# Storing a block's output from the residual's buffer, and transposing the next block's first chunk one half tile sooner

## The chip, the cores and the metric

The kernel runs on one core of a Trainium2 chip. Its time is device time in microseconds. The kernel before takes 1905.79 us, the median of three runs (1905.21 to 1907.05). A TensorE matmul of the granted full clock (2.4 GHz) is the unit in which most of the time goes.

## The reference

One layer of a hybrid decoder block over 4096 positions with 1024 channels, float32, batch 1:

```
h    = rms_norm(x, norm_g) * (1 + scale(c)) + shift(c)      # adaLN
proj = h @ w_in                                             # u, z_pool, q, k, v, o, z, gates
pool = (trailing means over 2/4/8/16 of u, minus u) @ w_pool * ls * silu(z_pool)
q, k = silu(causal conv of width 4)
hm   = mLSTM(q, k, v, gates), 4 heads of 128, chunks of 128 positions, in sequence
mix  = concat(pool, rms_norm(hm) * mh_norm_g * sigmoid(o) * silu(z))
out  = rms_norm(x + gate(c) * (mix @ w_out), final_g)
```

## The kernel before

The sequence is cut into 8 blocks of 512 positions, and a block into 4 chunks of 128. Block 0 is written out by itself (it also splits the weights), blocks 1 to 6 are a loop, and block 7 is written out again, without preparing a next one. Every large product is made in three matmuls from operands split into a high and a low part (`split3`, L465 to L469). Each engine has its own instruction list, in the order in which the code is written; semaphores order the engines among each other. All DMAs are issued by SP, one after another, so a DMA that waits keeps back those written behind it.

A block goes like this. TensorE computes v and the gates from eight units of weights (`v_part`), first four units for the first two chunks, then the rest; the second part waits until the last low part of the block's input is there (`h_lo`). Then come 16 tiles (q, k, z, o), of 24 matmuls each, in the accumulators acc0 and acc1 by turns, and then, per chunk, the pool tiles u and zp between the mLSTM's small products. VectorE's part of a chunk is `heads(j)` (it divides numerator by denominator and signals `h_ready`), `update_c(j)`, `head_var`, `head_norm`, and for the pool branch `y_low` (signals `y_lo`).

The output stage of a block has eight half tiles (chunk j, 512 of the 1024 columns each). `out_m(i)` adds the 12 matmuls of the mLSTM half, `out_p(i)` the 12 of the pool half, into the accumulator i % 2. `out_m(i)` waits until VectorE has emptied it (`acc_free`). Between them `prep_next(p)` transposes half a chunk of the next block's input (4 transposes) from `x_in` into num0 or num1; its first call waits for `h_ready` of chunk 3, because `heads(3)` reads these banks. VectorE then runs `add_residual(i)` (accumulator plus the loaded input row, into `x_res`), `prep_full` (scale and shift of the transposed chunk), `prep_var` and `prep_scale` for the next input chunk, `out_var(j)` and `out_norm(j)`. ScalarE squares, GpSimd takes the root. ScalarE (L748) and GpSimd (L966) split the prepared chunk into high and low.

`x_in` and `x_res` hold two chunks each. `load_x(b+1, c)` fills `x_in` when the transposes of chunk c-2 are done (`x_T`). `load_res(b, j)` fills `x_res[j % 2]` with the input rows of chunk j, and `store(b, j)` writes the normed chunk out. At the end of a block SP has, in this order: weights for the next block, `load_x(2)`, `store(0)`, one unit of weights, `load_x(3)`, `load_res(2)`, `store(1)`, `load_res(3)`, `store(2)`, `store(3)`. The normed chunk lies in `normed`, which is the memory of qT: q is no longer needed then, and the next block's first q tile waits until the stores are through.

Of the kernel before, what the change touches and what calls it, by code (L numbers as in the profile page):

```python
# [34 lines left out]
P = 128  # L35
# [3 lines left out]
BLK = 512  # L39
NB = SEQ // BLK  # L40
NC = BLK // P
# [59 lines left out]
def build(nc, x, c, norm_g, w_ada, b_ada, w_in, b_gates, conv_w, conv_b, w_pool, ls_pool, mh_norm_g,  # L101
# [3 lines left out]
    with ExitStack() as ctx:  # L105
        def sb(name, shape, dt=F32):
            return ctx.enter_context(nc.sbuf_tensor("sb_" + name, shape, dt))
# [4 lines left out]
        def sem(name):  # L112
            return ctx.enter_context(nc.semaphore(name))
# [13 lines left out]
        qT, kT, oz = sb("qT", [P, NH, BLK]), sb("kT", [P, NH, BLK]), sb("oz", [P, NH, BLK])  # L127
# [11 lines left out]
        x_in = sb("x_in", [P, 2, D])  # L139
        x_res = sb("x_res", [P, 2, D])  # L140
        full = [dmat, k_w]
        normed = qT[:, :, :].rearrange("p (a h) n -> p a (h n)", a=2)
        junk = tanh[:, :].bitcast(BF16)
        fg = sb("fg", [P, D])
        wpool = q_in
# [28 lines left out]
        o_sq, o_var, o_rs = sb("o_sq", [P, 2]), sb("o_var", [P, 2]), sb("o_rs", [P, 2])  # L174
# [56 lines left out]
        stored = [sem("stored0"), sem("stored1")]  # L231
        o_sq_done, o_var_done, o_rs_done, o_ready = (
            sem("o_sq_done"), sem("o_var_done"), sem("o_rs_done"), sem("o_ready"))
# [10 lines left out]
        def reach(eng, sem, value):  # L244

            if not (isinstance(value, int) and value <= 0):
                eng.wait_ge(sem, value)
# [34 lines left out]
        def _(sp):  # L282
# [65 lines left out]

            def load_res(b, j):

                reach(sp, o_ready, b * NC + (j - 1))
                sp.dma_start(x_res[:, j % 2, :], x[0, bass.ds(b * BLK + j * P, P), :]).then_inc(res_loaded[j % 2], 16)

            def store(b, j):
                sp.wait_ge(o_ready, b * NC + (j + 1))
                sp.dma_start(out[0, bass.ds(b * BLK + j * P, P), :], normed[:, j % 2, :]).then_inc(stored[j % 2], 16)

            sp.dma_start(cst[:, :], consts[:, 0:K_END]).then_inc(cst_loaded, 16)
            sp.dma_start(warm[:, :, :].rearrange("p g n -> p (g n)"), consts[:, K_END:K_END + K_COR]).then_inc(misc_loaded, 16)
# [104 lines left out]
        def _(pe):  # L464
# [52 lines left out]
            def one_block(b, last_block, first=False):  # L517
                def acc_wait(name, i):
                    t = TASK[name, i]
                    reach(pe, acc_free[t % 2], b * (TASKS // 2) + t // 2)  # L520
                    return acc[t % 2]
# [158 lines left out]
                def out_m(i):  # L680

                    j, cols = i // 2, slice(512 * (i % 2), 512 * (i % 2) + 512)
                    dst = acc_wait("out", i)
                    if first and i == 0:
                        pe.wait_ge(wout_lo_done, KT)
                    if i % 2 == 0:
                        pe.wait_ge(m_lo, b * NC + (j + 1))
                    for h in range(NH):
                        split3(dst[:, :], mixm_hi[:, j % 2, h, :], mixm_lo[:, j % 2, h, :],
                               wo_hi[:, NH + h, cols], wo_lo[:, NH + h, cols], h == 0, False)  # L690
# [12 lines left out]
                def prep_next(p):  # L703
                    if not last_block:
                        if p == 0:
                            pe.wait_ge(h_ready, b * NC + NC)
                        prep(b + 1, p)

                out_m(0)
                out_m(1)  # L710
                prep_next(0)
                prep_next(1)
                for i in range(8):
                    if i > 1:
                        out_m(i)
                    out_p(i)
                    if i == 1:
                        hm_transposed(3)
                    if i in (2, 4, 6):
                        prep_next(i)  # L720
                        prep_next(i + 1)
# [298 lines left out]
        def _(dve):  # L1020
            V = nc.vector
# [4 lines left out]
            def step(ins):  # L1026

                ins.then_inc(dve_step, 1)
                count[0] += 1
                did(dve_step, base[0] + count[0])  # L1030
# [5 lines left out]
            def in_turn():  # L1036

                reach(dve, *latest[0])
# [128 lines left out]
            def one_block(b, last_block, first=False):  # L1167
# [112 lines left out]
                for t, (name, i) in enumerate(TILES[:16]):  # L1280
                    in_turn()
                    if name in "qk":

                        sh = shifted[:, t % 2, :]
                        tap = [par[:, C_CW + 8 * n + t:C_CW + 8 * n + t + 1] for n in range(CW)]
                        step(V.tensor_copy(sh[:, HALO - 3:HALO], halo_qk[:, t, :]))
                        dve.wait_ge(acc_free[t % 2], b * (TASKS // 2) + (t // 2 + 1))
                        step(V.tensor_scalar(acc_cv[:, HALO:], sh[:, HALO:], tap[3], par[:, C_CB + t:C_CB + t + 1],
                                             ALU.mult, ALU.add))
                        for n in (2, 1, 0):  # L1290
                            in_turn()
                            ins = V.scalar_tensor_tensor(acc_cv[:, HALO:], sh[:, HALO - 3 + n:HALO - 3 + n + BLK], tap[n],  # L1292
                                                         acc_cv[:, HALO:], ALU.mult, ALU.add)
                            if n:
                                step(ins)
                            else:
                                ins.then_inc(conv_done, 1)
                                did(conv_done, b * 8 + (t + 1))
                        V.tensor_copy(halo_qk[:, t, :], sh[:, HALO + BLK - 3:HALO + BLK]).then_inc(shifted_free, 1)
                        dve.wait_ge(tanh_ready, b * TANHS + (t + 1))  # L1300
                        dve.wait_ge(conv_done, b * 8 + (t + 1))
                        if t == 0:
                            for i2 in range(2):
                                reach(dve, stored[i2], 16 * 2 * b)
                        V.scalar_tensor_tensor((qT if name == "q" else kT)[:, i, :], tanh[:, :], 1.0, acc_cv[:, HALO:],
                                               ALU.add, ALU.mult).then_inc(qk_ready, 1)
                        did(qk_ready, b * 8 + (t + 1))
                    elif name == "z":

                        src, free = acc_wait(name, i)  # L1310
                        dve.wait_ge(tanh_ready, b * TANHS + (t + 1))
                        V.scalar_tensor_tensor(oz[:, i, :], tanh[:, :], 1.0, src[:, :], ALU.add, ALU.mult).then_inc(free, 1)  # L1312
                        did(free, b * (TASKS // 2) + (TASK[name, i] // 2 + 1))
                    else:

                        src, free = acc_wait(name, i)
                        dve.wait_ge(tanh_ready, b * TANHS + (t + 1))
                        V.tensor_tensor(oz[:, i, :], tanh[:, :], oz[:, i, :], ALU.mult).then_inc(free, 1)  # L1318
                        did(free, b * (TASKS // 2) + (TASK[name, i] // 2 + 1))
                    if t == 0:  # L1320
                        log_gates()
                    if t == 2:
                        running_max()
                    if t == 4:
                        maxima()
                    if t == 6:
                        exponents()
                    if t == 8:
                        wide_rows()
                    if first and t > WOUT_TILE and t - WOUT_TILE <= KT:  # L1330
                        wout_low(t - WOUT_TILE - 1)
                    if first and 0 <= t - WOUT_TILE < KT:
                        wout_scale(t - WOUT_TILE)
                    if first and 0 <= t - FOLD_TILE - 1 < 2 * NH:
                        f = t - FOLD_TILE - 1
                        in_turn()
                        dve.wait_ge(fold_hi, f + 1)
                        V.tensor_tensor(mixm_lo[:, f % 2, :, :], num[1][:, :].rearrange("p (k n) -> p k n", n=P),
                                        mixm_hi[:, f % 2, :, :].bitcast(F32), ALU.subtract).then_inc(fold_lo, 1)
                        did(fold_lo, f + 1)  # L1340
# [174 lines left out]
                def out_norm(j):  # L1515
                    in_turn()
                    dve.wait_ge(o_rs_done, b * NC + (j + 1))
                    reach(dve, stored[j % 2], 16 * (b * 2 + j // 2))
                    V.scalar_tensor_tensor(normed[:, j % 2, :], x_res[:, j % 2, :], o_rs[:, j % 2:j % 2 + 1], fg[:, :],  # L1519
                                           ALU.mult, ALU.mult).then_inc(o_ready, 1)  # L1520
                    did(o_ready, b * NC + (j + 1))

# [58 lines left out]
```

## Time and profile before

| | |
|---|---|
| median of three runs | 1905.79 us |
| the profiled execution | 1905.21 us, its span 1903.4 us |
| TensorE matmul busy | 1819.3 us, 96% |
| TensorE weight load busy | 1552.0 us, 82% |
| VectorE busy | 1077.3 us, 57% |
| ScalarE busy | 470.2 us, 25% |
| GpSimd busy | 236.4 us, 12% |
| DMA, moved over the span | 324.32 MB, 170 GB/s |

Busy time is the union of an engine's instructions; matmuls overlap, so 96% says that there is nearly always one under way. The setup takes the first slices of the span; from then on one block follows another every 224 us, and the blocks 1 to 6 look alike. Output stages end near 331, 555, 780, 1004, 1229, 1453, 1677 and 1900 us. Times of rows are microseconds from the start of the span.

### The profile page before, as it was taken

Reading aid. Unit: us, or ns where it says so; the run is one execution under the profiler, and the core shown is the slowest. Engines: PE = TensorE matmul, PEld = TensorE weight load, DVE = VectorE, ACT = ScalarE, POOL = GpSimd, SP = SyncE. Lnnn points to the kernel's source line nnn. Section 1 sums busy time; section 2 is a strip of 40 time slices with the busy share of each in tenths; the row PEclk is TensorE's granted clock in tenths of the full one; section 3 lists DMA queues with packets and bytes.
Section 4 is the critical chain, followed back from the end, with each engine's and each line's share of the span. In section 5 each row is a group of like instructions: output and inputs, shape, how many; then the busy total and the mean of one; then the engine's idle time right before and its main releaser. Section 6 shows DMA issues by size and latency. Waiting matters only on the chain.

```text
span 1903.4 us, 27224 instructions
## 1 busy us (share of the span) xinstructions
PE 1819.3 (96%) x9505; PEld 1552.0 (82%) x9505; DVE 1077.3 (57%) x2453; ACT 470.2 (25%) x970; POOL 236.4 (12%) x213
## 2 busy tenths in 40 slices
PE   2797999999999999999999999999999999999998
PEld 1676888988888888888889888888888888898886
DVE  7677586454745366372764637544573627646373
ACT  1134432212312122221222122221221212222221
POOL 0443213000120002100020000300012000210000
PEclk9999999999999999999999999999999999999999
DMA  9598952665235652456425563266524564256521
GB/s 298 172 302 266 308 182 78 203 195 201 90 134 190 203 183 80 156 188 210 152 72 188 189 201 121 89 209 191 194 74 163 189 212 150 87 170 193 169 100 67
DMA packets 131499, 324.32 MB, mean 170 GB/s; under 512 B 11724, under 2 KB 49316, under 8 KB 131364
## 3 DMA queue, kind: packets, MB, share of 16 engines
q1 hardware_dynamic: 131364, 322.53, 51.3%
q8 instruction: 84, 1.38, 0.3%
q14 instruction: 51, 0.42, 0.1%
HBM read 276.28 MB, written 46.20 MB: 169 GB/s over the span
## 4 chain that ended last, share of the span: by engine, by line
issue 53%; PE 17%; DVE 14%; DMA 7%; POOL 2%; ACT 2%; SPq 1%; DVEq 0%; POOLq 0%; ACTq 0%
PE ps_acc L467 5%; PE ps_acc L469 4%; PE ps_acc L468 4%; DMA w_kept<-sb_w_split 2%; DMA sb_x_in<-x 2%; DVE sb_dmat L1063 2%; DVE sb_k_w L1063 2%; DVE sb_x_res L1505 1%; DMA sb_x_res<-x 1%; DVE sb_qT L1519 1%; POOL sb_h_rs L972 1%; DVE sb_mixm_lo L1418 1%; DVE sb_x_in L1045 1%; DMA sb_w_raw<-w_in 1%; POOL sb_hT_lo L966 1%
## 5 line engine op out<-in xcount | busy, mean ns | idle before, releaser
L467 PE MATMUL ps_acc<-sb_hT_hi,sb_w_split 128*128 128x512 f32 x1536 | 603.7, 393 | 0.0
L468 PE MATMUL ps_acc<-sb_hT_lo,sb_w_split 128*128 128x512 f32 x1536 | 599.5, 390 | 0.0
L469 PE MATMUL ps_acc<-sb_hT_hi,sb_w_split 128*128 128x512 f32 x1536 | 599.5, 390 | 0.0
L469 PEld LDWEIGHTS ps_acc<-sb_hT_hi,sb_w_split 128*128 128x128 f32 x1536 | 289.0, 188 | 61.6
L468 PEld LDWEIGHTS ps_acc<-sb_hT_lo,sb_w_split 128*128 128x128 f32 x1536 | 289.2, 188 | 59.2
L467 PEld LDWEIGHTS ps_acc<-sb_hT_hi,sb_w_split 128*128 128x128 f32 x1536 | 289.5, 188 | 58.5 <-POOL sb_w_split L960 0.3
L972 POOL TENSOR_TENSOR sb_h_rs<-sb_h_var,sb_mhalf 128x4 f32<-128x4 f32 x32 | 32.4, 1013 | 1122.5 <-DVE sb_h_var L1384 1122.5
L1292 DVE SCALAR_TENSOR_TENSOR sb_acc_cv<-sb_shifted,sb_par,sb_acc_cv 128x512 f32<-128x512 f32 x192 | 146.2, 762 | 6.8
L467 PE MATMUL ps_acc<-sb_wo_hi,sb_mixm_hi 128*128 128x512 f32 x256 | 103.8, 406 | 3.7 <-DVE sb_x_res L1505 3.7
L1318 DVE TENSOR_TENSOR sb_oz<-sb_tanh,sb_oz 128x512 f32<-128x512 f32 x32 | 22.2, 693 | 147.1 <-ACT sb_tanh L856 147.1
L467 PE MATMUL ps_acc<-sb_wo_hi,sb_mixp_hi 128*128 128x512 f32 x256 | 100.4, 392 | 3.3 <-DVE sb_mixp_lo L1403 3.3
L469 PE MATMUL ps_acc<-sb_wo_hi,sb_mixm_lo 128*128 128x512 f32 x256 | 100.1, 391 | 0.0
L468 PE MATMUL ps_acc<-sb_wo_lo,sb_mixm_hi 128*128 128x512 f32 x256 | 99.8, 390 | 0.0
L469 PE MATMUL ps_acc<-sb_wo_hi,sb_mixp_lo 128*128 128x512 f32 x256 | 99.8, 390 | 0.0
L468 PE MATMUL ps_acc<-sb_wo_lo,sb_mixp_hi 128*128 128x512 f32 x256 | 99.6, 389 | 0.0
L846 ACT ACTIVATE sb_tanh<-sb_acc_cv 128x512 f32<-128x512 f32 x64 | 40.6, 634 | 171.5 <-DVE sb_acc_cv L1292 171.4
L960 POOL TENSOR_TENSOR sb_w_split<-sb_w_raw,sb_w_split 128x512 fp32r<-128x512 f32 (+1 forms) x48 | 66.1, 1380 | 128.7 <-ACT sb_w_split L739 128.7
L467 PE MATMUL ps_kv<-sb_w_split,sb_hT_hi 128*128 128x256 f32 x256 | 73.0, 285 | 6.8 <-POOL sb_w_split L960 3.9
L1505 DVE TENSOR_TENSOR sb_x_res<-ps_acc,sb_x_res 128x512 f32<-128x512 f32 x64 | 44.3, 692 | 62.2 <-PE ps_acc L469 40.0
L1192 DVE TENSOR_TENSOR sb_g_pre<-ps_sco,sb_bg 128x8 f32<-128x8 f32 x8 | 1.3, 167 | 128.0 <-PE ps_num L469 128.0
L1312 DVE SCALAR_TENSOR_TENSOR sb_oz<-sb_tanh,ps_acc 128x512 f32<-128x512 f32 x32 | 22.0, 689 | 90.4 <-ACT sb_tanh L852 90.3
L875 ACT ACTIVATE sb_tanh<-sb_hm 128x128 bf16<-128x128 f32 x128 | 38.2, 300 | 139.9 <-DVE sb_hm L1366 139.9
(220 smaller groups left out, 2950.1 us busy)
## 6 DMA issues: line engine op xcount, KB each, us to landing
sb_w_split<-w_kept SPq DMA_DIRECT2D x344, 512.0 KB, 3.6
sb_w_split<-w_kept SPq DMA_DIRECT2D x56, 520.0 KB, 4.1
w_kept<-sb_w_split SPq DMA_DIRECT2D x40, 512.0 KB, 5.9
sb_x_res<-x SPq DMA_DIRECT2D x34, 512.0 KB, 5.6
out<-sb_qT SPq DMA_DIRECT2D x32, 512.0 KB, 2.9
sb_x_in<-x SPq DMA_DIRECT2D x30, 512.0 KB, 5.8
sb_w_raw<-w_in SPq DMA_DIRECT2D x48, 256.0 KB, 4.5
w_kept<-sb_w_split SPq DMA_DIRECT2D x8, 520.0 KB, 4.8
```

The lines of the kernel that those rows point to most:

```text
L467: pe.matmul(dst, st_hi, mv_hi, start=start, stop=False)
L468: pe.matmul(dst, st_hi, mv_lo, start=False, stop=False)
L469: return pe.matmul(dst, st_lo, mv_hi, start=False, stop=stop)
L846: act.activation(tanh[:, :], acc_cv[:, HALO:], ACT.Tanh, scale=0.5).then_inc(tanh_ready, 1)
L875: last = act.activation(junk[:, chunk(h)], hm[:, h, :], ACT.Square, accum_out=h_sq[:, h:h + 1])
L960: nc.gpsimd.tensor_tensor(w_split[:, m % RING, lo], w_raw[:, m % RING, lo], w_split[:, m % RING, hi].bitcast(F32), ALU.subtract).then_inc( ...
L972: nc.gpsimd.tensor_tensor(dst, src, mhalf[:, 0:n], ALU.pow).then_inc(done, 1)
L1063: last = V.tensor_scalar(full[p % 2][:, i, :], num[p % 2][:, chunk(i)], gain[:, k:k + 1], shift[:, k:k + 1], ALU.mult, ALU.add)
L1292: ins = V.scalar_tensor_tensor(acc_cv[:, HALO:], sh[:, HALO - 3 + n:HALO - 3 + n + BLK], tap[n], acc_cv[:, HALO:], ALU.mult, ALU.add)
L1312: V.scalar_tensor_tensor(oz[:, i, :], tanh[:, :], 1.0, src[:, :], ALU.add, ALU.mult).then_inc(free, 1)
L1318: V.tensor_tensor(oz[:, i, :], tanh[:, :], oz[:, i, :], ALU.mult).then_inc(free, 1)
L1505: V.tensor_tensor(x_res[:, j % 2, s], src[:, :], x_res[:, j % 2, s], ALU.add).then_inc(free, 1)
```

## The change

The normed chunk is written back into `x_res`, and the stores read it there. `load_res(b, j)` now waits until the store of the chunk two before it has landed (`stored`), where it waited for that chunk's norm (`o_ready`). VectorE's waits for `stored` are gone, in `out_norm` and at the first q tile. On TensorE `prep_next(0)` and `prep_next(1)` stand ahead of `out_m(1)`.

```
-        normed = qT[:, :, :].rearrange("p (a h) n -> p a (h n)", a=2)
...
             def load_res(b, j):
-                reach(sp, o_ready, b * NC + (j - 1))
+                reach(sp, stored[j % 2], 16 * (b * 2 + j // 2))
                 sp.dma_start(x_res[:, j % 2, :], x[0, bass.ds(b * BLK + j * P, P), :]).then_inc(res_loaded[j % 2], 16)

             def store(b, j):
                 sp.wait_ge(o_ready, b * NC + (j + 1))
-                sp.dma_start(out[0, bass.ds(b * BLK + j * P, P), :], normed[:, j % 2, :]).then_inc(stored[j % 2], 16)
+                sp.dma_start(out[0, bass.ds(b * BLK + j * P, P), :], x_res[:, j % 2, :]).then_inc(stored[j % 2], 16)
...
                 out_m(0)
-                out_m(1)
                 prep_next(0)
                 prep_next(1)
+                out_m(1)
                 for i in range(8):
                     if i > 1:
                         out_m(i)
                     out_p(i)
...
                         dve.wait_ge(tanh_ready, b * TANHS + (t + 1))
                         dve.wait_ge(conv_done, b * 8 + (t + 1))
-                        if t == 0:
-                            for i2 in range(2):
-                                reach(dve, stored[i2], 16 * 2 * b)
...
                 def out_norm(j):
                     in_turn()
                     dve.wait_ge(o_rs_done, b * NC + (j + 1))
-                    reach(dve, stored[j % 2], 16 * (b * 2 + j // 2))
-                    V.scalar_tensor_tensor(normed[:, j % 2, :], x_res[:, j % 2, :], o_rs[:, j % 2:j % 2 + 1], fg[:, :],
+                    V.scalar_tensor_tensor(x_res[:, j % 2, :], x_res[:, j % 2, :], o_rs[:, j % 2:j % 2 + 1], fg[:, :],
                                            ALU.mult, ALU.mult).then_inc(o_ready, 1)
```

TensorE before, in the loop of blocks 1 to 6, from the end of `out_m(1)` to the start of `out_p(0)` (`ps_num<-sb_cst,sb_x_in` are the transposes of `prep_next`):

```order
L468 MATMUL ps_acc<-sb_wo_lo,sb_mixm_hi 128x512
L469 MATMUL ps_acc<-sb_wo_hi,sb_mixm_lo 128x512
L475 ISA [waits h_ready]
L480 MATMUL ps_num<-sb_cst,sb_x_in 128x128 [waits x_scaled]
L480 MATMUL ps_num<-sb_cst,sb_x_in 128x128 x7
L467 MATMUL ps_acc<-sb_wo_hi,sb_mixp_hi 128x512 [waits y_lo]
```

The same engine now, from the end of `out_m(0)` to the start of `out_m(1)` (lines are one less than before):

```order
L467 MATMUL ps_acc<-sb_wo_lo,sb_mixm_hi 128x512
L468 MATMUL ps_acc<-sb_wo_hi,sb_mixm_lo 128x512
L474 ISA [waits h_ready]
L479 MATMUL ps_num<-sb_cst,sb_x_in 128x128 [waits x_scaled]
L479 MATMUL ps_num<-sb_cst,sb_x_in 128x128 x7
L466 MATMUL ps_acc<-sb_wo_hi,sb_mixm_hi 128x512 [waits acc_free1]
```

The wait for `h_ready` and the eight transposes have moved ahead of the 12 matmuls of `out_m(1)`, and these now stand right ahead of `out_p(0)`.

SP before, in the same loop, from `load_x(3)` on:

```order
L347 DMA sb_x_in<-x 128x1024
L352 ISA [waits o_ready]
L352 DMA sb_x_res<-x 128x1024
L355 REGISTER_ALU
L356 DMA out<-sb_qT 128x1024 [waits o_ready]
L352 ISA [waits o_ready]
L352 DMA sb_x_res<-x 128x1024
```

SP now:

```order
L346 DMA sb_x_in<-x 128x1024
L246 ISA
L351 ISA [waits stored0]
L351 DMA sb_x_res<-x 128x1024
L354 REGISTER_ALU
L355 DMA out<-sb_x_res 128x1024 [waits o_ready]
L351 ISA [waits stored1]
L351 DMA sb_x_res<-x 128x1024
```

The order of the DMAs is the same; the two residual loads wait for the landing of a store that stands ahead of them.

## Rows read from the trace of the kernel before

**Rows 1.** Waits of TensorE from 150 us: waited for, total us, times, longest.

```profile
PE ps_acc L467 <- DVE sb_x_res L1505: 3.7, 6, 0.9
PE ps_acc L467 <- DVE sb_mixp_lo L1403: 3.3, 6, 0.6
```

**Rows 2.** Timeline of TensorE, block 1: start us, us, instruction, idle before.

```profile
508.22 0.39 PE L467 MATMUL ps_acc<-sb_wo_hi,sb_mixm_hi 128*128 128x512 f32 x1
...
510.94 1.03 PE L480 MATMUL ps_num<-sb_cst,sb_x_in 128*128 128x128 f32 x8
512.53 0.50 PE L467 MATMUL ps_acc<-sb_wo_hi,sb_mixp_hi 128*128 128x512 f32 x1 [0.55 <-DVE sb_mixp_lo L1403]
...
515.38 0.39 PE L467 MATMUL ps_acc<-sb_wo_hi,sb_mixp_hi 128*128 128x512 f32 x1
...
524.04 1.03 PE L480 MATMUL ps_num<-sb_cst,sb_x_in 128*128 128x128 f32 x8
524.83 0.48 PE L467 MATMUL ps_acc<-sb_wo_hi,sb_mixm_hi 128*128 128x512 f32 x1
...
527.64 0.39 PE L467 MATMUL ps_acc<-sb_wo_hi,sb_mixp_hi 128*128 128x512 f32 x1
...
543.20 0.50 PE L467 MATMUL ps_acc<-sb_wo_hi,sb_mixm_hi 128*128 128x512 f32 x1 [0.90 <-DVE sb_x_res L1505]
...
560.94 0.28 PE L467 MATMUL ps_kv<-sb_w_split,sb_hT_hi 128*128 128x256 f32 x1
```

**Rows 3.** Timeline of VectorE, block 1's output stage.

```profile
509.07 0.76 DVE L1366 TENSOR_TENSOR sb_hm<-ps_num,sb_rden 128x256 f32<-128x256 f32 x2
...
540.16 0.15 DVE L1052 TENSOR_SCALAR sb_x_var<-sb_x_sq 128x1 f32<-128x1 f32 x1 [8.10 <-ACT sb_tanh L743]
...
542.45 0.69 DVE L1505 TENSOR_TENSOR sb_x_res<-ps_acc,sb_x_res 128x512 f32<-128x512 f32 x1 [0.22 <-PE ps_acc L469]
...
552.43 0.69 DVE L1505 TENSOR_TENSOR sb_x_res<-ps_acc,sb_x_res 128x512 f32<-128x512 f32 x1 [2.27 <-DMA sb_x_res<-x]
```

**Rows 4.** Timeline of ScalarE, block 1: the squares of the next input's chunks 2 and 3.

```profile
521.67 1.06 ACT L743 ACTIVATE sb_tanh<-sb_x_in 128x1024 bf16<-128x1024 f32 x1
...
538.98 1.06 ACT L743 ACTIVATE sb_tanh<-sb_x_in 128x1024 bf16<-128x1024 f32 x1 [5.65 <-DMA sb_x_in<-x]
```

**Rows 5.** Timeline of SP, block 1: issue of store(0), load_res(2), store(1), load_res(3).

```profile
531.27 0.37 SPq L356 DMA_DIRECT2D out<-sb_qT  x1
...
533.16 0.35 SPq L352 DMA_DIRECT2D sb_x_res<-x  x1
547.85 0.36 SPq L356 DMA_DIRECT2D out<-sb_qT  x1
548.41 0.33 SPq L352 DMA_DIRECT2D sb_x_res<-x  x1
```

**Rows 6.** Us from issue to landing: DMAs of 512.15, 531.27, 532.52, 533.16 and 562.11.

```profile
sb_x_in<-x SPq DMA_DIRECT2D x1, 512.0 KB, 3.4
...
out<-sb_qT SPq DMA_DIRECT2D x1, 512.0 KB, 3.0
...
sb_x_in<-x SPq DMA_DIRECT2D x1, 512.0 KB, 6.4
...
sb_x_res<-x SPq DMA_DIRECT2D x1, 512.0 KB, 7.0
...
out<-sb_qT SPq DMA_DIRECT2D x1, 512.0 KB, 2.7
```

**Rows 7.** Timeline of all engines, block 0: the heads' end and out_p(0).

```profile
285.78 0.76 DVE L1366 TENSOR_TENSOR sb_hm<-ps_num,sb_rden 128x256 f32<-128x256 f32 x2
...
289.23 0.50 PE L467 MATMUL ps_acc<-sb_wo_hi,sb_mixp_hi 128*128 128x512 f32 x1
```

**Rows 8.** Busy time by stretch, block 0; behind the engines PEclk, DMA share, GB/s.

```profile
263.00:265.00 2.00, 0.22 (x2) 0.03 (x1) 1.97 (x2) 0.00 (x0) 1.03 (x1) 1.00 0.08 31
265.00:267.00 2.00, 1.64 (x11) 1.56 (x12) 1.83 (x8) 0.00 (x0) 0.00 (x0) 0.96 0.57 231
```

**Rows 9.** Timeline of GpSimd, block 1: the last low part for block 2.

```profile
556.99 1.97 POOL L966 TENSOR_TENSOR sb_hT_lo<-sb_k_w,sb_hT_hi 128x512 fp32r<-128x512 f32 x1 [0.27 <-ACT sb_hT_hi L748]
```

More of the change, by code:

```diff
@@ L141, in build @@
         full = [dmat, k_w]
-        normed = qT[:, :, :].rearrange("p (a h) n -> p a (h n)", a=2)
         junk = tanh[:, :].bitcast(BF16)
@@ L349, in load_res @@
             def load_res(b, j):
-                reach(sp, o_ready, b * NC + (j - 1))
+                reach(sp, stored[j % 2], 16 * (b * 2 + j // 2))
                 sp.dma_start(x_res[:, j % 2, :], x[0, bass.ds(b * BLK + j * P, P), :]).then_inc(res_loaded[j % 2], 16)
@@ L355, in store @@
                 sp.wait_ge(o_ready, b * NC + (j + 1))
-                sp.dma_start(out[0, bass.ds(b * BLK + j * P, P), :], normed[:, j % 2, :]).then_inc(stored[j % 2], 16)
+                sp.dma_start(out[0, bass.ds(b * BLK + j * P, P), :], x_res[:, j % 2, :]).then_inc(stored[j % 2], 16)
             sp.dma_start(cst[:, :], consts[:, 0:K_END]).then_inc(cst_loaded, 16)
@@ L709, in one_block @@
                 out_m(0)
-                out_m(1)
                 prep_next(0)
                 prep_next(1)
+                out_m(1)
                 for i in range(8):
@@ L1301, in one_block @@
                         dve.wait_ge(conv_done, b * 8 + (t + 1))
-                        if t == 0:
-                            for i2 in range(2):
-                                reach(dve, stored[i2], 16 * 2 * b)
                         V.scalar_tensor_tensor((qT if name == "q" else kT)[:, i, :], tanh[:, :], 1.0, acc_cv[:, HALO:],
@@ L1517, in out_norm @@
                     dve.wait_ge(o_rs_done, b * NC + (j + 1))
-                    reach(dve, stored[j % 2], 16 * (b * 2 + j // 2))
-                    V.scalar_tensor_tensor(normed[:, j % 2, :], x_res[:, j % 2, :], o_rs[:, j % 2:j % 2 + 1], fg[:, :],
+                    V.scalar_tensor_tensor(x_res[:, j % 2, :], x_res[:, j % 2, :], o_rs[:, j % 2:j % 2 + 1], fg[:, :],
                                            ALU.mult, ALU.mult).then_inc(o_ready, 1)
```

## The prediction

> **What bounds the kernel now.** I read the list of waits first. After the setup TensorE hardly ever stops, so only its waits can be won or lost, and in the output stage it has two kinds: for the low part of the pooled mix (`y_lo`) ahead of `out_p(0)`, 3.3 us in 6 blocks, and for a freed accumulator (`acc_free`, released by `add_residual(4)`) ahead of `out_m(6)`, 3.7 us in 6 blocks [rows 1]. Then the TensorE timeline of block 1's output stage, where the reader sees both stalls and the price of a group: 12 matmuls take 508.22 to 510.94 = 2.72 us in full flow, 2.85 right behind a stall (512.53 to 515.38) and 2.81 right behind eight transposes, which themselves take 0.79 (524.04, 524.83, 527.64) [rows 2]. Then VectorE in the same stretch, to see when `heads(3)` is done and what its later idle times hang on [rows 3], and last ScalarE, the DMA queue and the landings, to see which transfer ends these idle times [rows 4 to 6].
>
> Two facts come out of that. First, `heads(3)` ends at 509.07 + 0.76 = 509.83 [rows 3], while `out_m(0)` ended at 508.22 [rows 2]. Second, VectorE stands still for 8.10 us until 540.16 because ScalarE's square waits for the fourth input chunk (538.98) [rows 3, 4]. That load stands in SP's queue behind the first store (531.27), so the chain store, `load_x(3)`, square, `prep_scale`, `add_residual(4)` (542.45 + 0.69 = 543.14) is what holds TensorE until 543.20 [rows 2, 3, 5].
>
> **The order on TensorE: the transposes before `out_m(1)`.** `prep_next(0)` waits for `h_ready`, the end of `heads(3)`. Before, `out_m(1)` ran while VectorE got there. Now TensorE reaches the wait at 508.22 and stands until 509.83: 1.6 us. Behind it come the eight transposes, `out_m(1)` and `out_p(0)`; the old wait for `y_lo` is then covered, since `out_m(1)` ends after 512.5. From the end of `heads(3)` to the start of `out_p(0)` it was 512.53 - 509.83 = 2.70 us [rows 2, 3]. It becomes 0.06 to wake (as 512.53 stands behind its releaser) + 0.79 + 2.81 = 3.66. `out_p(0)` no longer starts behind a stall, which gives back 2.85 - 2.72 = 0.13. Net 3.66 - 2.70 - 0.13 = 0.83 us per block. Block 0 has the same distance (285.78 + 0.76 = 286.54 to 289.23, 2.69 us) [rows 7], and blocks 1 to 6 repeat to a few hundredths; block 7 prepares nothing. 7 x 0.83 = **+5.8 us**. VectorE's heads do not move, because what stands ahead of them on VectorE is not touched. Not shown is a TensorE that wakes at this very wait: it is a wait of its own ahead of the transposes. The longest that TensorE stands behind a releaser in these rows is 0.06 us; as the upper end I take 0.3 us more per block, a little over twice the 0.13 of a restart. So +5.8 to +7.9; I take the low end, to which all the rows are near. Below 5.8 it can come only if `heads(3)` ends sooner, which is rival D.
>
> What the earlier transposes could bring: `x_T` frees the input buffer some 1.3 us sooner, so `load_x(2)` starts sooner. But it landed 3.4 us after its issue, near 515.6 [rows 6], and the square that reads it ran at 521.67 behind other work of ScalarE [rows 4]. And `prep_full(0)` stands on VectorE behind `add_residual(0)`, which waits for `out_p(0)`. Both gains are zero; ends 0 and 0.
>
> Does a stall of 1.6 us cost TensorE its clock? In block 0 it stood from 263.2 to 265.4 and the granted clock was 1.00 and then 0.96, the 2.4 GHz level but for a moment [rows 8]. I take nothing.
>
> **The store out of `x_res`, and the residual load that waits for it.** The norm writes where it reads, 1024 elements as before; I take no change of its time. `load_res(2)` was issued at 533.16; the store of 531.27 landed 3.0 us later, at 534.3 [rows 5, 6]. So it starts at 534.4, 1.2 us late. It landed after 7.0 us (540.2) between three other transfers; it is needed at 542.45, and even 7.0 us again gives 541.4. Free. What it does to `load_x(3)`, issued just ahead of it, is the open point. Between 534.3 and 538.9 two transfers landed, 2.3 us each, and then the residual only 1.3 us after [rows 6]: so the residual had part of the bandwidth while `load_x(3)` was under way. The chain behind `load_x(3)` releases TensorE at `out_m(6)`, six times, 3.7 us plus 6 x 0.14 of restart [rows 1]. Ends: nothing, and all of it, 4.5. By the row nearest to it, the residual's start moves 1.2 of the 6.4 us and half the sharing is late in them; I take 0.3 us per block, 6 x 0.3 = 1.8, less what a short stall can't give: **-1.6 us**.
>
> A rule bears on this. The Trainium skill (DMA: Bandwidth & Descriptors, "Queues, rings and completion order") says that on each DMA engine descriptors are consumed in ring order, though they may finish writing out of order. By it a load issued behind `load_x(3)` takes nothing from it, and the 1.6 us would not come; the 1.3 us between the two landings in this trace speaks against a strict reading.
>
> `load_res(3)` waits for the second store instead of its norm. Store issued at 547.85; alone such a store lands in 2.7 and such a load in 3.4 us [rows 6]. So 547.85 + 2.7 + 0.1 + 3.4 = 554.05, where `add_residual(6)` now starts at 552.43 [rows 3]: 1.6 us late, 1.3 after the 0.3 of above. Behind it VectorE, ScalarE and GpSimd hand on the last chunk of the next block's input; the last low part ends at 556.99 + 1.97 = 558.96 and TensorE asks for it at 560.94 [rows 9, 2]. 558.96 + 1.3 = 560.3 against 560.6 (0.3 earlier, since the stall shrank): just hidden. With 3.0 and 3.9 us it would be 561.4, a stall of 0.5. Slacks of the blocks differ by some tenths; ends 0 and 3 us, I take **+0.4**. Queued behind on SP are the stores 2 and 3 and the next block's weights; they move by the same 1.3 us, which the ring of five slots covers. In block 7 the residuals have 5 us and more to spare. The wait on `stored` that VectorE loses in the first q tile ended long before: nothing.
>
> **Sum.** 5.8 - 1.6 + 0.4 = +4.6 us. The profiled execution took 1905.2 us (span 1903.4), so 1909.8; the median of the runs is 0.6 above it: 1910.4.
>
> **Rivals.**
> A. No sharing: `load_x(3)` lands as before (two loads of one queue in order). Then +5.8 + 0 = 1911.6. For it: both are on one queue. Against: the 1.3 us. The rule quoted above is this case.
> B. Full sharing: `load_x(3)` lands 0.9 us or more sooner and the stalls at `out_m(6)` go: 5.8 - 4.5 + 0.2 = +1.5, 1907.3. For it: all four transfers run at once. Against: most of `load_x(3)`'s own time is past the residual's new start.
> C. Residual late: store and load need 3.0 and 3.9 us, and TensorE waits for the last input chunk in most blocks: 5.8 - 0.8 + 3 = +8, 1913.8. It decides from 2.0 us of delay on. For it: `add_residual(6)` waits for the DMA already, 2.27 us [rows 3].
> D. Faster: `h_ready` is not the last wait. If `heads(3)` ended by 508.9, the transposes and `out_m(1)` would be through by 512.5, when `y_lo` comes, and the new order would cost nothing; with B's gain of 4.5 the sum is -4.5 + 0.2, 1901.5. It decides at 508.9 against the 509.83 of the trace; nothing in the change moves VectorE there.
>
> **How the numbers follow.** Forecast 0.40, A 0.20, B 0.18, C 0.17, D 0.05. 0.2% (3.8 us) is about what a measurement of this kernel tells from no change. Of the forecast's own width (1908 to 1912.5) some three quarters lie beyond 3.8 us: slower 0.30 + 0.20 + 0.17 = 0.67; within 0.10 + 0.18 = 0.28; faster 0.05. The range from B to C, each with some tenths around it, is 1906.5 to 1914.2; it leaves D and the far ends out.
>
> **What would show it.** On TensorE an idle time of about 1.6 us ahead of the transposes in blocks 1 to 6 (0.9 in block 0), the wait for `y_lo` gone, 0.8 us net per block. At `out_m(6)` waits of 0.1 to 0.6 us (A: as before; B: none). ScalarE's square of chunk 3 starting 0.3 us sooner relative to the store. `add_residual(6)` waiting 3.5 to 4 us for its load. TensorE idle at the second half of the V stage: C. The forecast is wrong if TensorE has no new idle time before the transposes.

## The result, and the profile after

The changed kernel takes 1919.01 us, the median of six runs (1917.57 to 1919.97); before on the same chips took 1906.06 (1905.21 to 1907.05, six runs). The ratio is 1.0067, with an interval of 1.0056 to 1.0078: slower by 13.0 us. The direction is the one forecast, the time lies outside the range (1906.5 to 1914.2).

The page of the kernel after, its span and its engines' busy times:

```profile
span 1918.4 us, 27211 instructions
PE 1821.0 (95%) x9505; PEld 1552.6 (81%) x9505; DVE 1076.0 (56%) x2453; ACT 469.3 (24%) x970; POOL 235.2 (12%) x213
```

TensorE is busy 1.7 us longer than before and no other engine is; the rest of the 15 us of span was added as waiting. TensorE's waits after, from 150 us (the line waited for, total us, times, longest), to set beside [rows 1]:

```profile
PE ps_num L479 <- DVE sb_hm L1362: 10.2, 7, 1.6
PE ps_kv L466 <- issue: 6.1, 5, 1.4
PE ps_acc L466 <- DVE sb_x_res L1501: 3.1, 6, 0.6
```

The first is the wait for `h_ready` that was forecast, and the one for `y_lo` is gone. The third is the wait at `out_m(6)`, 0.6 us smaller. The second was in nobody's sum: five waits of up to 1.4 us ahead of a `ps_kv` matmul, the first of a V stage, and what it waited for is not named. The TensorE timeline of block 1 after, where all three stand (to compare with [rows 2]):

```profile
513.39 1.09 PE L479 MATMUL ps_num<-sb_cst,sb_x_in 128*128 128x128 f32 x8 [1.57 <-DVE sb_hm L1362]
514.24 0.48 PE L466 MATMUL ps_acc<-sb_wo_hi,sb_mixm_hi 128*128 128x512 f32 x1
...
517.08 0.39 PE L466 MATMUL ps_acc<-sb_wo_hi,sb_mixp_hi 128*128 128x512 f32 x1
...
547.17 0.50 PE L466 MATMUL ps_acc<-sb_wo_hi,sb_mixm_hi 128*128 128x512 f32 x1 [0.43 <-DVE sb_x_res L1501]
...
552.75 1.04 PE L479 MATMUL ps_num<-sb_cst,sb_x_in 128*128 128x128 f32 x8
...
560.60 0.38 PE L466 MATMUL ps_kv<-sb_w_split,sb_hT_hi 128*128 128x256 f32 x1 [1.37 <-issue]
```

In the kernel before the last transposes and the first matmul of the V stage stand 6.34 us apart (548.79 to 555.13), with no wait shown:

```profile
548.79 1.03 PE L480 MATMUL ps_num<-sb_cst,sb_x_in 128*128 128x128 f32 x8
...
555.13 0.37 PE L467 MATMUL ps_kv<-sb_w_split,sb_hT_hi 128*128 128x256 f32 x1
```

After, 552.75 to 560.60 are 7.85 us. Between the two stands the jump back to the head of the loop over blocks 1 to 6. Of the seven passages from a block to the next, five make this jump (out of blocks 1 to 5), and just these five have the stall; block 0 falls into the loop and block 6 out of it, with 6.33 us from the last transposes to the V stage after block 6. I cut all timelines at three marks and summed over blocks 0 to 6: from the first `out_m(0)` matmul to the transposes behind `out_p(1)` (part one, where the order was changed), and from there to the next V stage (part two). These transposes are the four small ones of `hm`, at 518.10 in block 1 before.

| | part one, us | part two, us | ratio to before, interval |
|---|---|---|---|
| before | 88.4 | 256.9 | |
| after | 95.2 | 262.6 | 1.0067 (1.0056 to 1.0078) |
| order only | 95.7 | 257.1 | 1.0034 (1.0022 to 1.0046) |
| buffer only | 88.3 | 263.2 | 1.0040 (1.0026 to 1.0053) |
| `load_res(2)` late | 88.4 | 257.5 | 1.0003 (0.9994 to 1.0011) |
| `load_res(3)` late | 88.8 | 263.9 | 1.0034 (1.0022 to 1.0047) |
| 0.5 MB more at the block's end | 88.8 | 265.0 | 1.0038 (1.0024 to 1.0052) |
| 1 MB more there | 88.8 | 267.4 | 1.0063 (1.0049 to 1.0076) |
| 0.5 MB more in the V stage | 88.9 | 258.9 | 0.9993 (0.9984 to 1.0002) |
| `prep_scale` later | 83.5 | 256.9 | 0.9968 (0.9956 to 0.9980) |
| after, `prep_scale` later | 90.1 | 263.0 | 1.0042 (1.0029 to 1.0056) |
| `load_x(3)` ahead of the store | 88.4 | 251.2 | 0.9960 (0.9946 to 0.9974) |
| after, `load_x(3)` ahead | 95.7 | 251.9 | 1.0005 (0.9996 to 1.0014) |
| both moves on before | 83.6 | 251.5 | 0.9934 (0.9920 to 0.9948) |

Part one grew by 6.8 us, in all seven blocks, and part two by 5.7, in blocks 1 to 5 alone: 12.5 of the medians' 13.0. Inside part two the way from the last transposes to the V stage grew at the five jumps by 1.51, 1.09, 1.22, 1.24 and 1.17 us, 6.2 in all, and 0.5 came back ahead of them, at `out_m(6)`. The other 2.5 us of the profiled span lie in block 0, whose first stages differ by up to 5.6 us between the profiled executions of these kernels (its `out_m(0)` starts between 279.83 and 285.39).

### The profile page after: what moved, and what is told of

Same layout as the page of the kernel before. It is cut to its first block, busy times and chain, and to the rows that moved or that the text cites. A ratio compares the mean times of both kernels' runs of the same rounds, so it can differ in the third digit from the quotient of the medians.

```text
span 1918.4 us, 27211 instructions
## 1 busy us (share of the span) xinstructions
PE 1821.0 (95%) x9505; PEld 1552.6 (81%) x9505; DVE 1076.0 (56%) x2453; ACT 469.3 (24%) x970; POOL 235.2 (12%) x213
## 3 DMA queue, kind: packets, MB, share of 16 engines
q8 instruction: 84, 1.38, 0.3%
## 4 chain that ended last, share of the span: by engine, by line
issue 53%; PE 18%; DVE 15%; DMA 6%; POOL 2%; ACT 2%; SPq 1%; DVEq 0%; POOLq 0%; ACTq 0%
PE ps_acc L466 5%; PE ps_acc L468 5%; PE ps_acc L467 5%; DMA sb_x_in<-x 2%; DVE sb_dmat L1062 2%; DVE sb_k_w L1062 2%; DVE sb_x_res L1501 1%; DVE sb_x_res L1514 1%; DMA sb_x_res<-x 1%; DVE sb_acc_cv L1291 1%; POOL sb_h_rs L971 1%; DMA sb_w_raw<-w_in 1%; DMA out<-sb_x_res 1%; DMA w_kept<-sb_w_split 1%; DVE sb_mixm_lo L1414 1%
## 5 line engine op out<-in xcount | busy, mean ns | idle before, releaser
L466 PE MATMUL ps_kv<-sb_w_split,sb_hT_hi 128*128 128x256 f32 x256 | 73.1, 286 | 13.2 <-issue 6.1
L467 PE MATMUL ps_kv<-sb_w_split,sb_hT_hi 128*128 128x256 f32 x256 | 72.4, 283 | 0.0
```

The lines of the kernel that those rows point to most:

```text
L466: pe.matmul(dst, st_hi, mv_hi, start=start, stop=False)
L467: pe.matmul(dst, st_hi, mv_lo, start=False, stop=False)
```

## The experiments

**The two halves of the change.** Order only is the kernel before with

```
 out_m(0)
-out_m(1)
 prep_next(0)
 prep_next(1)
+out_m(1)
```

> The kernel before with the transposes ahead of out_m(1) alone. Theory 1 (the change's 13 us are two terms: the wait for the heads, and the residual load that keeps back TensorE's instruction fetch at the loop's jump): only the first term, about 1.0 us in each of 7 blocks, +6.5 us, and no TensorE idle time at the start of the V stage. Rival (the idle time at the V stage comes from the new order on TensorE, whatever the loads do): +12 us and about 1.2 us idle at the start of the V stage after blocks 1 to 5.

1912.8 against 1905.68, and the waits:

```profile
PE ps_num L480 <- DVE sb_hm L1366: 10.7, 7, 1.6
PE ps_kv L467 <- issue: 0.5, 2, 0.3
```

7.1 us, where 6.5 were expected. Its cost is in part one; at the jumps it leaves 0.5 us, where before has 0.3. Buffer only is the changed kernel with `out_m(1)` back ahead of `prep_next(0)`.

> The change without the new order on TensorE: stores from x_res, residual loads behind the stores. Theory 1: the second term alone, 5 loop passes x about 1.1 us = +5.7 us, less up to 2 us at out_m(6). Rival (the V stage's idle time comes from the order): within 2 us of the kernel before. My prediction's case B (unshared load_x(3)): -4 us.

1913.11, and the waits:

```profile
PE ps_kv L466 <- issue: 6.0, 5, 1.5
PE ps_acc L466 <- DVE sb_x_res L1501: 3.8, 6, 0.8
```

The new stall belongs to the buffer, and the wait at `out_m(6)` is that of before: the half that was to bring 1.2 us (-1.6 and +0.4) costs 7.4. The two halves together are 14.5 us against 13.0 for the change, within the intervals: they add up.

**Which of the two residual loads.** The kernel before, with only chunk 2 (q = 0) or only chunk 3 (q = 1) handled as after:

```
 def load_res(b, j):
-    reach(sp, o_ready, b * NC + (j - 1))
+    if j % 2 == q: reach(sp, stored[j % 2], 16 * (b * 2 + j // 2))
+    else: reach(sp, o_ready, b * NC + (j - 1))
...
-normed[:, j % 2, :]
+(x_res if j % 2 == q else normed)[:, j % 2, :]
```

> The kernel before, in which only chunks 0 and 2 are normed into x_res and stored from there, so that only load_res(2) waits for a store. Theory 1: nothing lost at the loop's jump; TensorE's wait at out_m(6) shrinks by 0.1 to 0.3 us a block, -1 us (between -2 and 0). Rival (the later load_res(2) frees load_x(3) wholly): the waits at out_m(6) go, -4 us. Third view (load_res(2) is what holds back the tail): slower by several us.

> The kernel before, in which only chunks 1 and 3 are normed into x_res and stored from there, so that only load_res(3) waits for a store. Theory 1: TensorE idle 1.0 to 1.4 us at the start of the V stage after blocks 1 to 5, +6 us, and the 16 KB of instructions fetched right behind the load's data. Rival (it is the later load_res(2), or both together): within 2 us of the kernel before.

With q = 0 it is 1906.88, no difference, and `out_m(6)` waits as before:

```profile
PE ps_acc L470 <- DVE sb_x_res L1508: 3.8, 6, 0.8
```

With q = 1 it is 1912.03 and the stall is there in full, with the order on TensorE untouched:

```profile
PE ps_kv L470 <- issue: 6.2, 5, 1.4
...
556.27 0.38 PE L470 MATMUL ps_kv<-sb_w_split,sb_hT_hi 128*128 128x256 f32 x1 [1.39 <-issue]
```

So `load_res(3)` alone makes it. But the V stage does not read the residual, and its first half does not read the chunk prepared last. What it does share with the load are the DMA engines. The timeline of SP after, block 1 (issue of store(0), `load_x(3)`, `load_res(2)`, store(1), `load_res(3)`):

```profile
535.67 0.37 SPq L355 DMA_DIRECT2D out<-sb_x_res  x1
...
536.93 0.46 SPq L346 DMA_DIRECT2D sb_x_in<-x  x1
...
538.88 0.34 SPq L351 DMA_DIRECT2D sb_x_res<-x  x1
551.82 0.36 SPq L355 DMA_DIRECT2D out<-sb_x_res  x1
554.62 0.33 SPq L351 DMA_DIRECT2D sb_x_res<-x  x1
```

The last was issued 0.38 us before the last transposes in the kernel before (548.41 to 548.79) and is now issued 1.87 us behind them. Busy time by stretch after (five engines, PEclk, DMA share, GB/s), around its data:

```profile
555.00:556.00 1.00, 1.00 (x6) 0.84 (x5) 0.00 (x0) 0.00 (x0) 0.00 (x0) 1.00 0.46 82
556.00:557.00 1.00, 1.00 (x6) 0.84 (x5) 0.00 (x0) 0.00 (x0) 0.00 (x0) 1.00 0.91 336
557.00:558.00 1.00, 1.00 (x6) 0.80 (x5) 0.00 (x0) 0.00 (x0) 0.00 (x0) 1.00 0.32 123
```

The data run until 557.7, and there one packet of another queue starts. The DMA queues after from 557.5 to 557.75 (packets, MB, share), and below those of before from 552.0 to 552.25:

```profile
q8 instruction: 1, 0.02, 23.1%
q1 hardware_dynamic: 3, 0.00, 4.3%
```

```profile
q8 instruction: 1, 0.02, 23.4%
q1 hardware_dynamic: 1, 0.00, 0.2%
```

It is a packet of 16 KB that fetches instructions. In both kernels the V stage begins 2.9 us after its start (557.71 to 560.60, 552.21 to 555.13). Before, the load's data were through at 552.0 and the packet came 3.4 us after the last transposes; after, it starts where the data end, 4.97 us after them. That the queue is TensorE's is read from its rhythm: in the trace of before some 160 to 310 of TensorE's instructions lie between two of its packets, except at the five jumps, where two packets come 3.0 to 3.5 us apart. This gave a theory to test: **data in flight at the jump hold back the fetch of TensorE's next instructions**, whoever reads the data. The changed kernel holds a comparison of its own. Block 6 ends without the jump and without such a packet in this stretch; the same load's data flow there, 3.0 to 5.0 us behind the last transposes (1685.52), and the V stage starts 6.33 us behind them, as ever:

```profile
1688.50:1690.50 2.00, 2.00 (x11) 1.65 (x10) 0.00 (x0) 0.00 (x0) 0.00 (x0) 1.00 0.71 242
```

**Data that nobody reads.** The kernel before with one more copy of 0.5 MB from x to a DRAM scratch per block, behind `load_res(3)`:

```
 load_res(b, 3)
+reach(sp, extra_done, b * 16)
+sp.wait_ge(stored[1], 16 * (b * 2 + 1))
+sp.dma_start(extra[:, 0:D], x[0, bass.ds(b * BLK, P), :]).then_inc(extra_done, 16)
```

> The kernel before plus one DMA of 512 KB per block (input rows to a scratch tensor in device memory, which nobody reads), issued when store(1) has landed, where load_res(3) stands in the changed kernel. No engine waits for it but SP, a block later. Theory 1 (data in flight at the jump keeps back TensorE's instruction fetch): idle time at the start of the V stage after blocks 1 to 5 as in the changed kernel or longer, +5 to +10 us. Rival (the fetch waits because the residual load or add_residual is late): nothing, within 1.5 us.

1914.95 against 1907.58. The waits:

```profile
PE ps_kv L473 <- POOL sb_hT_lo L972: 3.6, 2, 1.9
PE ps_kv L473 <- issue: 2.8, 2, 1.6
```

7.4 us, within the 5 to 10 expected, and the same stall in four of the five jumps (8.21, 7.74, 8.42 and 8.10 us from the last transposes to the V stage). In three of these the packet started 5.2 to 5.6 us behind the transposes. In the one of 7.74 it started in time, after 3.46 us, but took 2.5 us among the data instead of some 0.9. In the fifth jump it also started in time, took 1.5 us and cost little (6.57). That two of the stalls are put down to GpSimd is the label only: the V stage's first half waits for the fourth of the eight low parts, which was written long before, and the label names a later one, which ended during the stall.

The same with two copies, 1 MB:

> The same with two such DMAs, 1 MB. Theory 1: the fetch comes behind both, some 1.5 to 1.8 us later than with one, 5 passes x 1.6 = +8 us more than with one. Second view (the fetch shares bandwidth with the data but doesn't queue behind it): less than 2 us more. Rival: nothing.

1921.18, which is 6.2 us more than with one copy: between the two views expected, and for a reason that neither had. The packet does not wait for the second copy: the jumps grow by little (8.33, 8.42, 7.68, 8.35, 8.60; 2.3 us in all). But here the stall has a second price. Waits, and the first stretches of the V stage after block 1:

```profile
PE ps_kv L474 <- POOL sb_hT_lo L973: 7.7, 4, 2.1
...
PE ps_kv L474 <- issue: 1.2, 1, 1.2
```

```profile
560.00:561.00 1.00, 1.00 (x8) 1.00 (x7) 0.19 (x1) 0.78 (x1) 0.52 (x1) 0.55 0.76 307
561.00:562.00 1.00, 1.00 (x6) 1.00 (x6) 0.15 (x1) 0.37 (x2) 0.29 (x1) 0.50 0.54 217
562.00:563.00 1.00, 1.00 (x7) 1.00 (x6) 0.65 (x1) 0.00 (x0) 0.26 (x1) 0.50 0.00 0
563.00:564.00 1.00, 1.00 (x8) 1.00 (x8) 0.63 (x1) 0.00 (x0) 0.00 (x0) 0.74 0.03 8
```

The granted clock is 0.50, the 1.2 GHz level, for some 3 us, and the first half of the V stage takes 7.71 us where it takes 6.18: 1.5 us, in three of the five blocks.

**The same data at another time.** The copy of 0.5 MB moved behind `store(b, 2)`, which issues it some 5 us into the next V stage:

> The kernel before plus the same extra DMA of 512 KB per block, but issued when store(2) has landed, some 5 us into the V stage, when TensorE has jumped. Theory 1 (only data in flight at the jump costs): no idle time at the start of the V stage, within 1.5 us of the kernel before; a little may come from unit 5 of the weights, which has 1.4 us to spare. Rival (the extra traffic costs wherever it stands): +5 to +7 us as with the extra DMA at the jump.

1907.0 against 1907.47, and the stall is gone:

```profile
PE ps_kv L473 <- issue: 0.5, 2, 0.3
```

The rival, that 4 MB more of traffic cost the time, falls: it is the moment. Part two is still 2.0 us above before's; the time does not show it. Of these 0.4 us lie at the jumps and 1.6 at `out_m(6)`, whose waits add up to 5.3 us instead of 3.7: `load_x(3)` took 6.4 us on average over blocks 1 to 6, and 6.1 before. The copies at the block's end do the same there (5.2 and 5.1 us). Why a copy elsewhere in the block slows this load was not tried.

**The cover of the two waits of before.** Two moves ask what the waits of [rows 1] are worth, each on both kernels. `prep_scale` later takes VectorE's work out of the way of `y_lo`:

```
-if j >= 2 and not last_block:
-    prep_scale(b + 1, j - 2)
+if j == 2 and not last_block:
+    prep_scale(b + 1, 0)
...
 head_norm(3)
+if not last_block:
+    prep_scale(b + 1, 1)
```

> The kernel before, with VectorE's prep_scale of the next block's chunk 1 moved from ahead of heads(3) to behind head_norm(3). heads(3) ends 0.8 us sooner (0.75 and the step between). Theory (TensorE waits at out_p(0) for y_lo, on VectorE's chain): the wait of 0.55 us in blocks 1 to 6 goes, with its restart 0.8 to 0.9 us a block, -5 us. Rival (y_lo depends on ScalarE's y_high, not on VectorE): within 1.5 us.

> The changed kernel with the same move of prep_scale. Theory 1 (TensorE stands at the transposes until heads(3) is done, 1.6 us in blocks 1 to 6): the idle time ahead of the transposes falls to 0.8 us, 7 x 0.8 = -5.5 us against the changed kernel, +7 to +8 us against the one before; the jump's 1.2 us stay. Rival (the transposes are held by something else, as the scaled input): no change against the changed kernel.

On the kernel before, 1900.77 against 1907.58 (6.8 us, where 5 were expected), and part one is 4.9 us shorter where the list of waits showed 3.3. On the kernel after, 1915.7; `heads(3)` ends sooner and the new wait halves, but the jumps stay:

```profile
PE ps_kv L466 <- issue: 6.0, 5, 1.3
PE ps_num L479 <- DVE sb_hm L1362: 5.2, 7, 0.8
```

The other, with `load_x(3)` issued ahead of the first store:

```
 load_x(b + 1, 2)
+load_x(b + 1, 3)
 store(b, 0)
 load_w(b, UNITS)
-load_x(b + 1, 3)
```

> The kernel before with load_x(3) issued ahead of store(0). Theory (the chain store(0), load_x(3), square, prep_scale, add_residual(4) holds TensorE at out_m(6)): VectorE's idle time of 8 us before the variance of chunk 3 falls to 3 us, the six waits at out_m(6) go with their restarts, -4 to -4.5 us. Rival (out_m(6) waits for the residual's own load then): -1 us or less.

> The changed kernel with load_x(3) issued ahead of store(0) instead of behind it, so VectorE's tail is some 5 us earlier and load_res(3) with it. Theory 1: the residual load's data are through before the jump, the 1.0 to 1.4 us at five V stages go (-6 us), and the waits at out_m(6) too (-3.5 us): +3 to +4 us against the kernel before, the cost of the order alone being 6.5. Rival (the buffer change costs something at the jump that isn't the time of its load): +8 us or more.

On before it takes the wait at `out_m(6)` away: 1900.45 against 1907.47 (7.0 us, where 4 to 4.5 were expected), part two 5.7 us shorter where 3.7 were shown. Part of VectorE's standstill of 8.10 us [rows 3] goes with it:

```profile
533.58 0.16 DVE L1052 TENSOR_SCALAR sb_x_var<-sb_x_sq 128x1 f32<-128x1 f32 x1 [2.48 <-ACT sb_tanh L743]
```

On after it gives 1907.67: by the two ratios some 12 us less than the changed kernel, and no more than before (+0.2 us, where 3 to 4 were expected), though all of the order's cost is still there. The waits:

```profile
PE ps_num L479 <- DVE sb_hm L1362: 10.7, 7, 1.6
...
PE ps_kv L466 <- POOL sb_hT_lo L965: 0.5, 2, 0.3
```

The jumps' stall is gone with the wait at `out_m(6)`: with `load_x(3)` early, the second chunk's norm, its store and `load_res(3)` all come sooner. In block 1 the load is issued 0.36 us ahead of the last transposes, as in the kernel before, and at all five jumps its data are through by 2.7 us behind them, before the packet starts.

**The best version.** Both moves on the kernel before:

> The kernel before with both: load_x(3) ahead of store(0), and prep_scale of chunk 1 behind head_norm(3). If the two are independent: the sum, -5.5 - 4.5 = -10 us, 1896 us; TensorE then has no wait left in the output stages. Rival (one makes the other's wait late again): -6 us.

1894.82 against 1907.47 (12.7 us, where 10 were expected), 0.66% faster than before and 1.3% than the changed kernel. The gains of the two moves add up (0.32 and 0.40%), and TensorE has no wait left in its output stages; what is named first from here on is in the mLSTM stage and at one jump:

```profile
PE ps_sco L626 <- DVE sb_oz L1411: 4.6, 7, 2.2
...
PE ps_kv L467 <- issue: 0.2, 1, 0.2
```

## Why the prediction was right in direction and wrong in size

**The order on TensorE: +5.8 forecast, +6.8 measured.** The mechanism is as written. The timeline of VectorE after shows `heads(3)` at

```profile
512.51 0.76 DVE L1362 TENSOR_TENSOR sb_hm<-ps_num,sb_rden 128x256 f32<-128x256 f32 x2
...
515.20 0.69 DVE L1399 TENSOR_TENSOR sb_mixp_lo<-sb_silu_zp,sb_mixp_hi 128x512 fp32r<-128x512 f32 x1 [0.35 <-ACT sb_mixp_hi L879]
...
558.31 0.69 DVE L1501 TENSOR_TENSOR sb_x_res<-ps_acc,sb_x_res 128x512 f32<-128x512 f32 x1 [4.18 <-DMA sb_x_res<-x]
```

It ends at 513.27. From there to `out_p(0)` at 517.08 are 3.81 us, where I had 3.66: 0.12 instead of 0.06 to wake, transposes 0.85 for 0.79, and 2.84 for 2.81. So 0.15 more a block, 0.83 + 0.15 = 0.98; the seven blocks give 6.8 / 7 = 0.97, and order only says the same in the time (7.1 us). `y_lo` (515.89) is covered with 1.2 us to spare. The term was mis-sized by 1 us, inside its own ends. Rival D did not come: `heads(3)` is the last wait. And the stall of 1.6 us cost no clock, as forecast: the granted clock is 1.00 behind all six. But the row on which that rested was read too short, and here luck helped. [rows 8] end at 267; the next stretches of the kernel before are

```profile
266.00:267.00 1.00, 1.00 (x8) 0.92 (x7) 0.86 (x7) 0.00 (x0) 0.00 (x0) 0.93 0.16 62
267.00:268.00 1.00, 1.00 (x3) 0.77 (x3) 0.96 (x4) 0.35 (x3) 0.00 (x0) 0.50 0.00 0
```

The clock was at the 1.2 GHz level until 270.2, and a matmul of 512 columns followed the one before it after 0.43 us instead of 0.23. So a stall of 2.1 us can cost the clock in this kernel, and 1.6 us were not shown to be safe by it.

**`load_res(2)` and `load_x(3)`: -1.6 forecast.** The gain did not come. In block 1, which I had read, `load_x(3)` landed after 5.9 us instead of 6.4; but over blocks 1 to 6 it took 6.10 us on average before (5.84 to 6.37), 6.04 after, and 6.14 with `load_res(2)` late and nothing else changed. The wait at `out_m(6)` follows this landing: 0.90 us with 6.37, 0.35 with 5.84. In all it fell from 3.7 to 3.1 us in the changed kernel, but it was 3.8 with `load_res(2)` late (time 1.0003) 3.8 with the whole buffer half, and 3.4 with the new order alone; so the 0.5 us cannot be put down to the later residual load. That is rival A: no run shows that the residual behind it takes anything from `load_x(3)`. Here the 1.3 us between the two landings misled me; two loads can land close together without the first having lost to the second. By the rule of the Trainium skill (DMA: Bandwidth & Descriptors, "Queues, rings and completion order"), that on each DMA engine descriptors are consumed in ring order, this was to be expected. These runs agree with it: 6.14 us against 6.10.

**`load_res(3)`: +0.4 forecast, +6.2 measured.** The chain of waits after has it as worked out:

```profile
551.82 2.63 DMA out<-sb_x_res
...
554.62 3.60 DMA sb_x_res<-x
```

against 2.7 and 3.4 forecast; `add_residual(6)` waited 4.18 us for it, forecast was 3.5 to 4. The last low part was there in time, too. In the timeline of GpSimd after:

```profile
562.87 1.98 POOL L965 TENSOR_TENSOR sb_hT_lo<-sb_k_w,sb_hT_hi 128x512 fp32r<-128x512 f32 x1 [0.26 <-ACT sb_hT_hi L747]
```

It ends at 564.85, and the second half of the V stage starts 6.18 us after 560.60, at 566.78. So rival C did not come. Without the 1.5 us of the jump's stall the second half would still have started after 564.85, at 565.3, so +0.4 was, for this mechanism, even too much. The step that failed is the question itself: "`load_res(3)` waits for the second store", and I followed it to those who wait for the load. I did not ask what else passes through the DMA engines at the moment to which its data moved. The trace of before held the answer: a queue of 84 packets and 1.38 MB, 16 KB each, on the page (it reads the same after),

```profile
q8 instruction: 84, 1.38, 0.3%
```

and in the timeline one jump of before that already lost a little to such a packet (it took 1.5 us there instead of 0.9; the data were through):

```profile
779.74 0.38 PE L467 MATMUL ps_kv<-sb_w_split,sb_hT_hi 128*128 128x256 f32 x1 [0.26 <-issue]
```

Shown: the load at this moment makes the stall (`load_res(3)` alone), its reader is not needed (the copy nobody reads), the amount of traffic is not the cause (the copy 5 us into the V stage), and an earlier load takes the stall away with all else kept (`load_x(3)` ahead on after). Worked out from the rows but not tried by itself: that the way is the 16 KB packet; no run moved this packet alone. What speaks for it is that at all 70 jumps of the 14 traces the V stage begins 1.7 to 2.1 us after the end of this packet, with and without a stall, and whether it started late or took long; and that the ends of blocks 0 and 6, which have no such packet behind the last transposes, take 6.33 to 6.34 us in every trace, also with 1 MB in flight.

**The sum.** Forecast 5.8 - 1.6 + 0.4 = 4.6; measured 6.8 + 5.7 = 12.5. The prediction failed at the term for `load_res(3)`, and the time fell outside the range with it. Of the 7.9 us between them 5.8 are the jump (6.2 for 0.4), 1.1 the gain at `out_m(6)` (0.5 for 1.6) and 1.0 the order. The chance of 0.67 for slower was well placed, but no rival had a price of this kind, and the range ended 5 us short.

## What to carry to other kernels

When a DMA is moved, ask two questions: who waits for its data, and what else passes the DMA engines while they flow; here TensorE's instruction fetch at a loop's jump is such a passenger, and with free queues it starts 3.3 to 3.9 us after the last transposes; data that flow then can hold it back. An idle time labelled "issue" at a jump is worth a look at the DMA queues 3 us earlier. And a small wait on the engine that sets the end was worth more than is shown: taking away 3.3 and 3.7 us of shown waits gave 4.9 and 5.7 us of the two parts and 6.8 and 7.0 us of the time, by one small vector operation later and one load earlier, without any new buffer. And before a row is taken as proof that nothing happens, read on past its end: the clock fell in the microsecond behind [rows 8].

## What the hardware showed that I had not expected

- A packet of 16 KB, 0.02 MB of 322, decides over 1.1 to 1.5 us at each jump when 0.5 MB of data flow in the same stretch; with 1 MB the jumps are only 0.5 us longer on average than with 0.5 MB.
- Whether TensorE's clock falls behind a stall is not told by its length alone. Behind the stalls of 1.0 to 1.6 us of the changed kernel it did not. The stall of 2.1 us of [rows 8] stands in block 0 of all 14 traces: behind it the clock fell to the 1.2 GHz level for some 3 us in six of them (before and after among these) and stayed at 2.4 GHz in eight, and a fall cost 1.6 us (from the stall's end to `out_m(0)` 17.48 us before, 15.86 with order only). At the jump it fell behind three of the four stalls of 1.8 to 2.1 us with 1 MB more, and not behind one of 1.9 us with 0.5 MB. What told the ones from the others was not tried.
- A shown wait understated the loss: 0.55 us shown ahead of `out_p(0)` in six blocks were worth 4.9 / 6 = 0.8 us each. The slower group behind a stall (2.85 for 2.72 us, [rows 2]) is a part of it; that the modelled ends of the matmuls hide the rest is likely but was not shown.
